# The state space of a second mixer in 64 chunks of 8 tokens instead of a scan over 512

## What is computed

```python
mag, ang = jnp.exp(lre * step), lim * step            # per group (32) and state (64)
a_re, a_im = mag * jnp.cos(ang), mag * jnp.sin(ang)
bu_re = jnp.einsum('blgc,gpc->blgp', uf, bb_re)       # 16 channels of a group to 64 states
bu_im = jnp.einsum('blgc,gpc->blgp', uf, bb_im)
# s[t] = a * s[t-1] + bu[t], complex, over the 512 tokens
y = (jnp.einsum('blgp,gcp->blgc', s_re, c_re) - jnp.einsum('blgp,gcp->blgc', s_im, c_im) + d_skip * uf)
z = jax.nn.gelu(y)
return z * jax.nn.sigmoid(z @ w_glu + b_glu)
```

## Time and profile before

| | us |
|---|---|
| median of 3 runs (lowest, highest) | 2529.92 (2527.82, 2539.81) |
| the profiled execution | 2535.4 |
| its span | 2533.6 |
| first turn's products to the attention loop's first matmul | 1688.45 to 1945.41 |

### The profile page before, as it was taken

The page is one execution under the profiler, slowest core; times in us unless marked ns, Lnnn a source line. Parts: engine busy times, 40 slices in busy tenths (PEclk is TensorE's granted clock), DMA queues, the critical chain, the costliest instruction groups (busy, mean ns, idle before and its releaser), DMA issues. The chain is left out here.

```text
span 2533.6 us, 30000 instructions
## 1 busy us (share of the span) xinstructions
PE 2152.2 (85%) x11186; PEld 1775.5 (70%) x11186; DVE 1390.0 (55%) x2500; ACT 879.8 (35%) x1490; POOL 589.5 (23%) x406
## 2 busy tenths in 40 slices
PE   6989897999997897989799999786677999468884
PEld 6888675888886887867588888574454778257663
DVE  3775544444443478354444443589985332458775
ACT  3443333322221443433322221232333441256662
POOL 2653210000000464320000000136665334100001
PEclk9998888999998898998799999797888999679997
DMA  3111101322210210100322220342112121378985
GB/s 130 68 34 34 34 1 51 134 99 99 99 66 31 77 65 34 34 18 1 133 100 100 99 99 17 129 163 83 50 35 77 52 95 43 125 304 343 372 342 216
DMA packets 46320, 258.85 MB, mean 102 GB/s; under 512 B 6896, under 2 KB 7024, under 8 KB 21744
## 3 DMA queue, kind: packets, MB, share of 16 engines
q1 hardware_dynamic: 43888, 248.77, 26.6%
q0 software_dynamic: 2304, 8.39, 0.9%
HBM read 224.63 MB, written 32.51 MB: 101 GB/s over the span
## 5 line engine op out<-in xcount | busy, mean ns | idle before, releaser
L415 PE MATMUL ffn_up<-f_hi,ffn_gu_hi 128*128 128x512 f32 x704 | 276.1, 392 | 15.0 <-DVE ffn_gu_lo L386 12.2
L415 PE MATMUL ffn_up<-f_lo,ffn_gu_hi 128*128 128x512 f32 x704 | 275.5, 391 | 0.0
L415 PE MATMUL ffn_up<-f_hi,ffn_gu_lo 128*128 128x512 f32 x704 | 275.3, 391 | 0.0
L1028 PE MATMUL fill_ps<-mix_whi,h_hi 128*128 128x256 f32 (+1 forms) x704 | 213.5, 303 | 15.3 <-DVE mix_wlo L914 8.3
L1028 PE MATMUL fill_ps<-mix_whi,h_lo 128*128 128x256 f32 (+1 forms) x704 | 204.3, 290 | 0.0
L1028 PE MATMUL fill_ps<-mix_wlo,h_hi 128*128 128x256 f32 (+1 forms) x704 | 203.9, 290 | 0.0
L369 DVE TENSOR_TENSOR ffn_silu<-ffn_silu,ffn_up 128x512 f32<-128x512 f32 x44 | 30.3, 688 | 293.1 <-ACT ffn_silu L341 293.1
L415 PEld LDWEIGHTS ffn_up<-f_hi,ffn_gu_hi 128*128 128x128 f32 x704 | 133.2, 189 | 44.4 <-DVE ffn_gu_lo L386 12.9
L381 DVE TENSOR_TENSOR x<-ffn_down,x 128x512 f32<-128x512 f32 x176 | 119.7, 690 | 80.5 <-PE ffn_down L430 79.7
L1028 PEld LDWEIGHTS fill_ps<-mix_whi,h_hi 128*128 128x128 f32 x704 | 140.9, 200 | 28.7 <-DVE mix_wlo L914 9.1
L616 POOL TENSOR_TENSOR mix_wlo<-mix_raw,mix_whi 128x1024 fp32r<-128x1024 f32 x56 | 141.2, 2532 | 70.0 <-ACT mix_whi L675 61.1
(11 more groups left out here) (410 smaller groups left out, 5519.5 us busy)
## 6 DMA issues: line engine op xcount, KB each, us to landing
moe_raw_gu<-in_w_e_gu SPq DMA_DIRECT2D x46, 1024.0 KB, 12.8
mix_raw<-in_w_mix SPq DMA_DIRECT2D x30, 1024.0 KB, 4.9
two_raw<-in_w_two SPq DMA_DIRECT2D x25, 1024.0 KB, 5.3
moe_raw_d<-in_w_e_down SPq DMA_DIRECT2D x23, 1024.0 KB, 9.1
ffn_raw_gu<-in_w_gate SPq DMA_DIRECT2D x22, 1024.0 KB, 5.0
ffn_raw_gu<-in_w_up SPq DMA_DIRECT2D x22, 1024.0 KB, 6.3
ffn_raw_d<-in_w_down SPq DMA_DIRECT2D x22, 1024.0 KB, 4.9
moe_in<-moe_empty SPq DMA_DIRECT2D x23, 512.0 KB, 8.8
```

Of the source, the lines that this page charges most:

```text
L415: last = nc.tensor.matmul(up_ps[m][b][:], ww[:, m, k, b * P:(b + 1) * P], aw[:, k, :], start=n == 0, stop=n == 3 * KD - 1)
L1028: last = nc.tensor.matmul(b[:, 0:cols], aw[:, k, t * P:(t + 1) * P], ww[:, k, 0:cols], start=k == 0 and n == 0, stop=k == KD - 1 and n == 2)
```

## The change

With chunks of 8 tokens, all that happens within a chunk is a product with a matrix, and only the state at the chunk's end is carried on: 64 steps of a scan with the factor of 8 tokens instead of 512 steps.

- VectorE makes the powers 0 to 8 of each rate, and from them the input matrices `in_m` (B times a power) and the output matrices `out_m` (C times a power). TensorE turns `in_m` round (`turn_in`) and makes the kernel of the chunk, C times a power times B (`within_chunk`), as a strip for each group.
- The layout must change: a chunk's 8 tokens times 16 channels shall lie on 128 partitions. u goes to memory (`u_save`) and comes back as `u_c` in 8 DMAs. The strips go to memory (`spread`) and come back as 8 shifted copies, which gives the triangular matrices `within`. The outputs go out in 8 DMAs (`y_save`) and come back in one, into `glu_in`.
- `inputs()` is now one block of 64 matmuls of 64 columns, `outputs(h)` two halves of 48. VectorE mixes, scans (32 scans of 64) and turns back all tiles at once, in a table of 64 chunks. The growing of tables and all of GpSimd's and ScalarE's part of the turns are gone.
- The order: all 24 token tiles of q, k and v and two gate tiles stand ahead of `outputs`; 14 gate tiles stand in the attention loop, half a tile in each of 28 steps, then w_glu, one tile a step. `make_y` comes at its steps 8 to 11, Gelu at step 13. All gates are stored with their bias alone, and their sigmoids stand behind the attention loop. The chunks are loaded in the order of use.
- The zeros for `moe_in` now come from a row of zeros in memory, in groups of 6, 6, 6 and 5.
- B and C are passed without their zero blocks (half the bytes); GpSimd clears the block diagonal form.

The diff, cut to its core:

```diff
-LONG = 64
...
+CH = 8
...
+NC = SEQ // CH
+POWERS = CH + 1
...
+EARLY_GATES = 2
+REL_UNIT_AT = {0: 2, 2: 3, 10: 4, 12: 5, 18: 6, 20: 7}
+REL_GATE = {n: (EARLY_GATES + n // 2, n % 2) for n in range(28)}
+REL_GLU = {28 + n: n for n in range(SQT)}
+REL_SPLIT_AT = {11: 4, 12: 8, 13: 12, 14: 16, 15: 20, 16: 24, 17: 28, 18: 32}
+REL_LOAD_AT = {1: (12,), 2: (13,), 3: (14,), 4: (15,), 5: (16,), 6: (17,), 7: (18,)}
+Z_AT, GELU_AT, Z_SPLIT_AT = 8, 13, 21
...
+                load(2)
+                load(3)
+                save_u(0)
+                save_u(1)
+                load(4)
+                save_u(2)
+                save_u(3)
+                sp.wait_ge(u_saved, 16 * SQT)
+                for i in range(CH):
+                    at = (CH - 1 - i) * GROUP
+                    sp.dma_start(u_c[at:at + GROUP], core.u_save.rearrange("(g c) (i n) -> i c g n", c=GROUP, i=CH)[i]).then_inc(u_in, 16)
+                load(5)
+                zero_rows(0, 6)
+                load(6)
+                zero_rows(6, 12)
+                sp.wait_ge(k_out, SQT)
+                sp.dma_start(core.spread.rearrange("(i r) n -> r i n", i=ST), spread).then_inc(k_saved, 16)
+                sp.wait_ge(k_saved, 16)
+                sp.wait_ge(in_turned, 2 * SQT)
+                for i in range(CH):
+                    rows = slice(i * GROUP, (i + 1) * GROUP)
+                    sp.dma_start(within[rows], core.spread.rearrange("(g c) n -> c g n", c=GROUP)[:, :, i * GROUP:i * GROUP + P]).then_inc(within_in, 16)
+                load(7)
+                zero_rows(12, 18)
+                load(8)
+                zero_rows(18, BLOCKS)
...
+                sp.wait_ge(turned_back, 2)
...
                     sp.dma_start(bias[j % 2], w["rel"][j]).then_inc(bias_in[j % 2], 16)
+                    if j == 1:
+                        load(11)
+                        sp.wait_ge(y_out, SQT)
+                        for i in range(CH):
+                            sp.dma_start(core.y_save.rearrange("(g c) (j n) -> j c g n", c=GROUP, j=CH)[i],
+                                         y_c[i * GROUP:(i + 1) * GROUP].rearrange("p (g n) -> p g n", g=GROUPS)).then_inc(y_saved, 16)
+                        sp.wait_ge(y_saved, 16 * CH)
+                        sp.dma_start(glu_in[:], core.y_save.rearrange("(f p) n -> p f n", p=P)).then_inc(y_back, 16)
...
+                    if c == 4:
+                        pool.wait_ge(v_made, 1)
+                        pool.wait_ge(b_out, 2)
+                        pool.wait_ge(x_out, 16)
+                        nc.gpsimd.memset(spread[:, :, 0:(CH - 1) * GROUP], 0.0).then_inc(spread_set, 1)
+                norm_root(0)
+                norm_root(1)
+                for h in range(2):
+                    split_lo(6, h)
+                norm_root(2)
+                for h in range(2):
+                    split_lo(7, h)
+                for h in range(2):
+                    split_lo(8, h)
+                norm_root(3)
+                for h in range(2):
+                    split_lo(9, h)
+                unit(0)
+                unit(1)
+                for h in range(2):
+                    split_lo(10, h)
...
+                    nc.scalar.copy(u_t[:, f, :].rearrange("p (i n) -> p i n", i=CH),
+                                   bank("u", f)[:].rearrange("p (n i) -> p i n", i=CH)).then_inc(u_out, 1)
...
+                for b in range(2 * SQT):
+                    evict_in(b)
+                for n in range(2 * TB, 3 * TB):
+                    evict_qkv(n)
+                split_both(6)
+                for b in range(SQT):
+                    evict_k(b)
+                square(1)
+                for n in range(3 * TB, 4 * TB):
+                    evict_qkv(n)
+                split_both(7)
+                square(2)
+                for n in range(4 * TB, 5 * TB):
+                    evict_qkv(n)
+                split_both(8)
+                square(3)
+                for n in range(5 * TB, 6 * TB):
+                    evict_qkv(n)
+                split_both(9)
+                for f in range(EARLY_GATES):
+                    evict_gate(f)
+                for u in range(2):
+                    evict_unit(u)
+                for b in range(SQT):
+                    evict_y(b)
+                split_both(10)
...
+                for f in range(KD):
+                    act.wait_ge(gate_out, f + 1)
+                    nc.scalar.activation(gate(f), gate(f), ACT.Sigmoid).then_inc(gate_done, 1)
...
+                shape, c_re, c_no, pr, pi, other = spread_over(out_m, c_t[:, 0], c_t[:, 1], POWERS)
+                tt(out_m[0], c_re, pr, ALU.mult)
+                tt(other, c_no, pi, ALU.mult)
+                tt(out_m[0], out_m[0], other, ALU.add)
+                tt(out_m[1], c_no, pr, ALU.mult)
+                tt(other, c_re, pi, ALU.mult)
+                nc.vector.tensor_tensor(out_m[1], out_m[1], other, ALU.subtract).then_inc(v_made, 1)
...
+                sum_squares(0)
...
+                dve.wait_ge(in_turned, 2 * SQT)
...
+                    if n == NC // 2:
+                        sum_squares(1)
...
+                sum_squares(2)
+                normalise(1)
+
+                dve.wait_ge(bu, 1)
+                half_cols = [slice(h * SEQ, (h + 1) * SEQ) for h in range(2)]
+                cos_f, sin_f = (v_.rearrange("p i n -> p (i n)") for v_ in table)
+                for h, cols in enumerate(half_cols):
+                    re, im = (in_ps[m][h][:] for m in range(2))
+                    nc.vector.tensor_tensor(part[0][:, cols], re, cos_f[:, cols], ALU.mult)
+                    nc.vector.tensor_tensor(part[1][:, cols], im, sin_f[:, cols], ALU.mult)
+                    nc.vector.tensor_tensor(part[2][:, cols], im, cos_f[:, cols], ALU.mult)
+                    nc.vector.tensor_tensor(part[3][:, cols], re, sin_f[:, cols], ALU.mult).then_inc(mixed, 1)
+                dve.wait_ge(mixed, 2)
+                nc.vector.tensor_tensor(part[0], part[0], part[1], ALU.add)
+                link(nc.vector.tensor_tensor(part[2], part[2], part[3], ALU.subtract))
+                for m in range(2):
+                    for i in range(ST):
+                        cols = slice(i * NC, (i + 1) * NC)
+                        last = nc.vector.tensor_tensor_scan(part[2 * m + 1][:, cols], bcast(mag_ch[:, i:i + 1], [P, NC]),
+                                                            part[2 * m][:, cols], 0.0, ALU.mult, ALU.add)
+                link(last)
+                nc.vector.tensor_tensor(part[0], part[1], cos_f, ALU.mult)
+                nc.vector.tensor_tensor(part[2], part[3], sin_f, ALU.mult)
+                nc.vector.tensor_tensor(part[1], part[1], sin_f, ALU.mult)
+                link(nc.vector.tensor_tensor(part[3], part[3], cos_f, ALU.mult))
+                v0, v1, v2, v3 = (v_.rearrange("p (i n) -> p i n", i=ST) for v_ in part)
+                nc.vector.memset(state[0][:, :, 0:1], 0.0)
+                nc.vector.memset(state[1][:, :, 0:1], 0.0)
+                nc.vector.tensor_tensor(state[0][:, :, 1:NC], v0[:, :, 0:NC - 1], v2[:, :, 0:NC - 1], ALU.subtract).then_inc(turned_back, 1)
+                nc.vector.tensor_tensor(state[1][:, :, 1:NC], v1[:, :, 0:NC - 1], v3[:, :, 0:NC - 1], ALU.add).then_inc(turned_back, 1)
+                normalise(2)
+                sum_squares(3)
+                normalise(3)
...
+                    if Z_AT <= n < Z_AT + SQT:
+                        make_y(n - Z_AT)
...
+                def within_chunk(b):
...
+                    if b >= 2:
+                        pe.wait_ge(k_out, b - 1)
+                    for n in range(4):
+                        i = 4 * b + n
+                        for m in range(2):
+                            last = nc.tensor.matmul(banks[6 + b % 2][0:2 * GROUP, n * P:(n + 1) * P], b_diag[:, m, i, :],
+                                                    out_m[m][:, i, 0:CH, :].rearrange("p d c -> p (d c)"), start=m == 0, stop=m == 1)
+                    last.then_inc(k_summed, 1)
...
+                def inputs():
...
+                    for i in range(ST):
+                        for m in range(2):
+                            for n in range(2):
+                                rows = slice(n * STATE, (n + 1) * STATE)
+                                last = nc.tensor.matmul(in_ps[m][i // 8][rows, (i % 8) * NC:(i % 8 + 1) * NC], in_t[m][:, i, rows],
+                                                        u_c[:, 2 * i + n, :], start=True, stop=True)
                     last.then_inc(bu, 1)
...
+                def outputs(h):
...
+                    for i in range(8 * h, 8 * h + 8):
+                        for n in range(2):
+                            rows = slice(n * STATE, (n + 1) * STATE)
+                            y = banks[6 + n][:, (i % 8) * NC:(i % 8 + 1) * NC]
+                            nc.tensor.matmul(y, within[:, 2 * i + n, :], u_c[:, 2 * i + n, :], start=True, stop=False)
```

(29 more changed lines are left out.)

542 lines of the change are left out of this document (218 added, 324 removed).

## The result

The changed kernel takes 2461.44 us (median of 4 runs, 2448.76 to 2462.54), before 2530.06 (2527.82 to 2539.81): a ratio of 0.9707, 95% interval 0.9688 to 0.9727. It is 68.6 us faster, where 96 were forecast. The time lies in the range, 27 us above the forecast value.

What follows compares the result with a forecast made beforehand. VectorE's turns were taken to bound the loop over 16 tiles, TensorE the attention loop. 141 us gained ahead, less the attention loop's growth from 107.6 to 152 and 1 in the tail, gave 96: 2529.9 - 96 = 2434 us, range 2412 to 2476.

Steps and rivals of the forecast that it cites:

- What bounded the kernel: VectorE limits the 254 us loop over 16 tiles of states through its turns; TensorE limits the 111 us attention loop.
- VectorE's sum: VectorE's new steps up to the tables: 44.3 us plus 12.9 of stalls, output matrices ready at 1700.0, table at 1725.4.
- TensorE's chain: From 1700 each step hangs on TensorE: within a chunk to 1709, inputs to 1722, four token tiles to 1733.5.
- The start of the mixing: VectorE begins mixing at 1740, 13 us after it had the table, behind ScalarE's split of chunk 7 and squared keys.
- Outputs: 96 matmuls, 192 records, 20.2 us: TensorE's outputs ahead of the attention loop, at 0.105 us a record, with 2 us more for copies.
- I take 0.9, 10 us: TensorE's mean clock over the 94 us ahead of the attention loop, adding 10 us: loop starts at 1804.
- The end of 22: Upper bound for clock loss ahead of the attention loop: the first loop's 0.81 would stretch 94 us by 22.
- Clock high: Rival, chance 0.17: TensorE's clock stays full and handing over is free; 10 us less, up to 5 from scans: 2421.
- Swaps late: Rival, chance 0.12: swap pieces through memory cost 100 ns, 26 us a swap, 33 us beyond cover: 2467.
- ScalarE or GpSimd pacing the attention loop: Rival, chance 0.10: the order of their queues costs 1 us a step in the attention loop, 36 us: 2470.
- Slower by the price of pieces: Rival, chance 0.04: short swap pieces eat the 96 us at 0.18 us each; at 0.22 the time is 2558.
- The clock of 1700 to 1800 at 0.85 to 1.0: Sign of a right prediction: TensorE's granted clock in that stretch, ahead of the attention loop.

Runs made afterwards that it cites:

- x_rows: Changed kernel with the strips read back in whole rows of 16 KB instead of pieces of 512 B (triangular matrices hold other values): 2457.8 us.
- x_loads: Changed kernel with three moves in GpSimd's, ScalarE's and SyncE's queues and chunks 8, 9 and 10 loaded earlier, outputs unpaired: 2448.3 us.
- x_dense: x_banks with two gate tiles taken from the attention loop and put among the outputs: 2436.9 us.
- x_all: Changed kernel with the two groups of each output tile side by side, two gate tiles among the outputs and three queue moves: 2452.9 us.
- x_fill: Changed kernel with two gate tiles taken out of the attention loop and put between the outputs in eighths: 2474.4 us.
- x_held: x_banks with gate tile 1 among the first half of the outputs, gate tile 2 among the second, units turned between the halves: 2446.9 us.
- x_queue: Changed kernel with GpSimd's roots behind splits, ScalarE's third squares ahead of chunk 7's split, chunk 7 loaded ahead of the strips' copies: 2468.1 us.
- x_banks: x_order with the outputs' second half in two other PSUM banks and the attention loop's first two scores ahead of the last copies: 2423.7 us.
- x_order: Changed kernel with each output tile's groups side by side, three queue moves, and chunks 8, 9 and 10 loaded ahead of zeros: 2425.9 us.

## Why the prediction was right, and where its size was off

*What bounded the kernel* was right: with the turns gone, 116.7 us are gone ahead of the attention loop (1945.4 to 1828.7; 141 were forecast), and 151.3 - 107.1 = 44.2 come back in it, where 44.5 were forecast. The tail was to cost 1 and cost nothing.

*VectorE's sum* held in its marks: output matrices, table and states within 3 us, with the stalls of 4.3 us for a chunk that GpSimd splits beside it. For the scans that was luck. The prediction took 0.3 us for each and argued from its rows that scans are not held by GpSimd. Alone they cost 0.19 each, 5.94 in all, and the split of chunk 7 added 4.3: two errors that cancel.

*TensorE's chain* held at its later marks, and partly by errors that cancel. The inputs cost 3.9 us and not 13.4, and the strips 6.0, not 6.7. Of the 12 us saved 8.0 went into the wait for the low half of chunk 6, which the later arrival would have hidden; the root ahead of it was not in the prediction. The second wait, 4.9 us to 1749.2 for the low half of chunk 7, was there with 2 (1745 to 1747). The outputs began at 1774.9 and not 1771.

*The start of the mixing*, 1740.28 for 1740, was met by luck. The forecast hung it on the token tiles that stand ahead of chunk 7's split in ScalarE's queue, done at 1733.5. They were done at 1721.1, and ScalarE then waited 13.2 us for chunk 7, whose load the prediction had put under cover.

*The failing step* is "Outputs: 96 matmuls, 192 records, 20.2 us", with "I take 0.9, 10 us" for the clock. In all 33 us were forecast from the outputs to the attention loop, and it took 53.8. First, the price: 0.105 a record came from a row of full 128 x 128 products standing together. The strips' products cost that when they stand together (0.22 each), but here they alternated with products on 64 rows: 0.945 a group at full clock, 30.2 us for 32, 10 more than forecast. Second, the clock: at 0.50 nearly all through, the stretch lost 53.8 - 30.2 - 1.2 = 22.4 us, not 10. The end of 22 stood in the text as a bound, from the first loop's 0.81, but spread over 94 us and tied to idle times; here TensorE was not idle. 10 + 12.4 and the later start of 3.9, less 1.6 of smaller terms, are the 24.7 us by which the attention loop starts late. The loop and the tail then gave back 3.3, and the forecast had taken off 5.5 us because the profiled execution of before lay above its median, where that of the changed kernel lies 0.4 below: together the 27 us.

*The rivals.* Clock high: no. Swaps late: at 73 ns a piece for the second one it came half true; chunk 7 was 13 us late, yet with longer pieces (x_rows) it came only 3.2 us sooner and the outputs 4.9. ScalarE or GpSimd pacing the attention loop: no. Slower by the price of pieces: no; two of the three swaps went at 30 and 38 ns. Per byte the pieces of 256 B cost no more here than those of 512 B.

*What would show it.* The mixing was held by the squares, as said, though by another reason behind them. The first score matmul came at 1828.7 and not near 1804. "The clock of 1700 to 1800 at 0.85 to 1.0" is wrong (0.82 over it, 0.50 from 1777.1), and one sign named for a wrong prediction was there: ScalarE waited 13.2 us for the DMA of chunk 7.

## What to carry to other kernels

When many large steps are replaced by few short ones, price a short product by the array form it stands next to: products on the two halves of the rows belong side by side, in two banks, and not between full ones. That was worth 20 to 22 us here, the largest single edit. And when a chain gets earlier, look up what its next partner's queue has ahead of the awaited step: the roots, then a weight chunk behind a swap, each hid the next, and only moving all of them paid.

## What the runs showed that was not expected

- The granted clock fell to half (1.2 GHz) with TensorE busy for the whole time, 2.3 us into the outputs of the changed kernel (1777.1), and stayed there for the 50 us that they still took. In the other runs with no gate work among the outputs it fell 3.6 (x_rows) to 5.4 us (x_loads) into them, in pairs or not. What sets the moment stays open. The Trainium skill's page "TensorE: Matmul & The Clock Gate", in the section on the clock gate, lists the half clock with idle; here only the wait of 1.2 us between the halves stood in it, and 0.34 us of idle time in the 23 us ahead of it.
- Outputs with gate products among them kept the full clock for 25 us (x_dense) and 14 us (x_all), but in x_fill they lost it after 2.5 us, and started at half clock they stayed there for 28 us (x_held).
- A scan of 64 columns costs 0.19 us in a row of such scans (x_queue), and 2.43 when GpSimd splits a weight chunk beside it. GpSimd's splits hold VectorE's scans as they hold its products and sums.
- 64 products of 64 columns with 64-column weights, written to the two halves of the partitions by turns, took 3.9 us, 0.06 each: less than a third of the price of those with 128.
- Pieces of 512 B read from strips of 960 B went at 73 ns each per engine, pieces of 256 B at 38 (from memory) and 30 (to memory, with the engines not always busy).
- The best version, x_banks, takes 2423.7 us, 0.9576 of before and 38 us less than the changed kernel; x_order, at 2425.9, cannot be told from it.
